# Transposing the probabilities ahead of the next unit's scores in a two-layer diffusion trunk

## The reference

```python
s_win = where(valid, einsum('bnqkgd,bnskd->bnkgqs', qb, kb) * scale, -inf)
s_ctx = einsum('bnqkgd,bckd->bnkgqc', qb, kc) * scale
p = softmax(concatenate([s_sink, s_ctx, s_win], axis=-1), axis=-1)
o = einsum('bnkgqc,bckd->bnqkgd', p_ctx, vc) + einsum('bnkgqs,bnskd->bnqkgd', p_win, vb)
```

## Time and profile before

| | |
|---|---|
| median of 3 runs | 1605.48 us (1605.39 to 1608.4) |
| the profiled execution | 1605.48 us, its span 1603.8 us |
| TensorE busy with matmuls | 1527.6 us, 95% of the span |
| TensorE busy with weight loads | 967.7 us, 60% |
| VectorE | 679.4 us, 42% |
| ScalarE | 314.5 us, 20% |
| GpSimd | 38.5 us, 2% |
| DMA | mean 230 GB/s |

### The profile page before, as it was taken

The page is one execution under the profiler, slowest core; times in us unless marked ns, Lnnn a source line. Parts: engine busy times, 40 slices in busy tenths (PEclk is TensorE's granted clock), DMA queues, the critical chain, the costliest instruction groups (busy, mean ns, idle before and its releaser), DMA issues. The chain is left out here.

```text
span 1603.8 us, 23021 instructions
## 1 busy us (share of the span) xinstructions
PE 1527.6 (95%) x9610; PEld 967.7 (60%) x9610; DVE 679.4 (42%) x1400; ACT 314.5 (20%) x721; POOL 38.5 (2%) x49
## 2 busy tenths in 40 slices
PE   5999989999999999989999999999999999899995
PEld 2764644754445446875556556776678888655553
DVE  1396776556655433451222126345533312611112
ACT  2121144321121100110111013234322111100011
POOL 0000000000000000000000020000000000000000
PEclk7999999999999999999999999999999999999998
DMA  9575411524525349379999986332115368899996
GB/s 367 186 242 180 140 43 53 133 69 142 185 92 180 138 172 355 139 278 402 411 396 395 401 344 226 114 99 67 40 43 168 127 254 314 312 426 429 420 410 289
DMA packets 127816, 368.08 MB, mean 230 GB/s; under 512 B 14237, under 2 KB 91319, under 8 KB 106972
## 3 DMA queue, kind: packets, MB, share of 16 engines
q1 hardware_dynamic: 118588, 344.86, 57.0%
q10 hardware_dynamic: 5392, 10.99, 2.3%
q0 software_dynamic: 3728, 10.71, 1.8%
HBM read 355.89 MB, written 12.98 MB: 230 GB/s over the span
## 5 line engine op out<-in xcount | busy, mean ns | idle before, releaser
L1304 PE MATMUL ps<-hT,ring 128*128 128x512 f32 (+1 forms) x768 | 258.5, 486 | 1.4 <-ACT arena L1774 1.4
L1177 PE MATMUL ps<-hT,ring 128*128 128x512 f32 (+1 forms) x544 | 207.7, 535 | 0.0
L1304 PEld LDWEIGHTS ps<-hT,ring 128*128 128x128 f32 x768 | 144.1, 190 | 98.1 <-issue 88.7
L1180 PE MATMUL ps<-ring,hT 128*128 128x256 f32 (+1 forms) x832 | 173.5, 365 | 6.5 <-DVE arena L2083 5.0
L1180 PEld LDWEIGHTS ps<-ring,hT 128*128 128x128 f32 x832 | 146.9, 190 | 30.6 <-issue 13.5
L1177 PEld LDWEIGHTS ps<-hT,ring 128*128 128x128 f32 x544 | 101.4, 191 | 87.1 <-issue 82.0
L1321 PE MATMUL ps<-arena,ring 128*128 128x512 f32 (+1 forms) x384 | 132.7, 486 | 0.0
L1467 PE MATMUL ps<-ring,arena 128*32 128x128 f32 (+2 forms) x1216 | 107.5, 343 | 2.8 <-DMA ring<-in_w_exp_gate 2.3
L1321 PEld LDWEIGHTS ps<-arena,ring 128*128 128x128 f32 x384 | 72.3, 190 | 47.8 <-issue 43.1
L1467 PE MATMUL ps<-arena 128*32 128x128 f32 (+1 forms) x1264 | 91.7, 328 | 1.9 <-DMA arena<-in_w_exp_up 1.2
L1467 PEld LDWEIGHTS ps<-ring,arena 128*32 128x32 f32 (+2 forms) x1216 | 66.5, 128 | 41.8 <-issue 24.8
(11 more groups left out here) (288 smaller groups left out, 1593.6 us busy)
## 6 DMA issues: line engine op xcount, KB each, us to landing
ring<-in_w_in SPq DMA_DIRECT2D x54, 1024.0 KB, 6.2
ring<-in_w_ada SPq DMA_DIRECT2D x48, 1024.0 KB, 5.1
arena<-in_w_exp_down SPq DMA_DIRECT2D x18, 2048.0 KB, 19.0
arena<-in_w_exp_up SPq DMA_DIRECT2D x15, 2048.0 KB, 17.2
ring<-in_w_exp_down SPq DMA_DIRECT2D x14, 2048.0 KB, 16.9
ring<-in_w_exp_gate SPq DMA_DIRECT2D x12, 2048.0 KB, 18.0
ring<-in_w_exp_up SPq DMA_DIRECT2D x12, 2048.0 KB, 17.0
hT<-in_w_exp_gate SPq DMA_DIRECT2D x10, 2048.0 KB, 18.3
```

The costliest lines, as they stand in the source:

```text
L1177: last = pe.matmul(ps[:, bank, 0:tok.stop - tok.start], w[:, k, at:at + width], hT[:, k, tok], start=(k == 0), stop=(k == KD - 1))
L1180: last = pe.matmul(ps[:, bank, 0:width], hT[:, k, P * tok:P * (tok + 1)], w[:, k, at:at + width], start=(k == 0), stop=(k == KD - 1))
L1304: last = pe.matmul(ps[:, 0, lo:TOK], kview(n)[:, k, P * (m % 2):P * (m % 2 + 1)], hT[:, k, lo:TOK], start=(k == 0), stop=(k == KD - 1))
```

## The change

In TensorE's `unit(n)` the transposes of unit n-1 now stand ahead of the scores of unit n. In VectorE's `unit(n)` the copy of those transposes (`keep_turned`) now stands ahead of the maxima. Nothing else is changed: no wait, no buffer, no plan. ScalarE's, GpSimd's and SyncE's programs are the same instruction for instruction.

```diff
@@ TensorE, unit(n)
                     if 2 <= n:
                         outputs(n - 2)
+                    if 1 <= n <= n_units[l]:
+                        turn(n - 1)
                     if n < n_units[l]:
                         scores(n)
-                    if 1 <= n <= n_units[l]:
-                        turn(n - 1)
@@ VectorE, unit(n)
                     if 2 <= n:
                         keep_output(n - 2)
+                    if 1 <= n <= n_units[l]:
+                        keep_turned(n - 1)
                     if n < n_units[l]:
                         maxima(n)
-                    if 1 <= n <= n_units[l]:
-                        keep_turned(n - 1)
```

## The result

The changed kernel is slower: 1620.05 us median of five runs (1618.65 to 1625.72), against 1608.4 of the kernel before on the same chips (1605.39 to 1610.51). The ratio is 1.0082, with a 95% interval of 1.0067 to 1.0096, some 13 us. The forecast was 1611.6 us in a range of 1606.5 to 1615.5. The sign was right. The size was less than half of what came, and the time lies outside the range.

What follows compares the result with a forecast made beforehand. The prediction took TensorE, busy 1527.6 of 1603.8 us, as the bound. Waits for the divide 4.95, bank copies 0.4 and 0.8 made 6.15 us on 1605.48: 1611.6 us, range 1606.5 to 1615.5.

Steps and rivals of the forecast that it cites:

- What bounds the kernel, and where the change acts: TensorE, busy 1527.6 of 1603.8 us, sets the end; the change acts in layer 0's `b` units, where transposes wait 5.4 us.
- Term s: Scores that filled TensorE's wait for the divide now follow it: 0.7 us with 256 keys, 1.1 with 512.
- term d: VectorE's copy ahead of the maxima makes the divide later: 0.35 us per unit with 256 keys, 0.6 with 512, adding up.
- The forecast's eight waits: Layer 0 transposes waiting for the divide at b0, b2, b3, b5, b6, b7, b9, b10, making TensorE 4.95 us later.
- Where the divide is long done, the two just change places and cost nothing.: In units whose transposes don't wait for the divide, swapping them with the scores costs TensorE nothing.
- the zero for the `a` units: TensorE has no wait in layer 0's `a` units and the copy's delay is hidden, so the change costs zero there.
- The forecast's own sign for layer 1: If layer 1 adds more than 1.5 us, its slack was smaller than the forecast took it for.
- The bank copies: TensorE waits longer for VectorE's copy L2083 because the maxima come later: 0.4 us at b13, 0.8 in layer 1.
- I keep one fall, as today.: TensorE's clock falls to half once, at b3, as before; a fall more or less at b7 is 1.5 us of range.
- One swap only: Rival, chance 0.17: VectorE's copy stays hidden, lateness doesn't add up, only b7's 1.1 us remains after b0; 1606.6 us.
- Faster: Rival, chance 0.04: VectorE's copy fits its idle time before the maxima, waits for L2083 go, -4.1 us; 1601.4 us.
- Lateness feeds itself: Rival, chance 0.15: second clock fall at b7, longer one at b3, bank copies in every late unit; 1614 to 1617 us.

Runs made afterwards that it cites:

- The kernel with the slack units alone: Changed order on both engines only in layer 0's `a` units and all layer 1 units, against the kernel before: ratio 1.0019, 3.1 us slower.

## Why the prediction was wrong

**What bounds the kernel, and where the change acts.** Right. TensorE's lateness in the mixers went to the end whole; the experts between neither absorbed nor added more than 1 us in the two profiles.

**Term s behind a wait, and term d.** Right in place and nearly in size. The forecast's eight waits came, the other eight units had none, and TensorE's idle time in the stretch grew by 4.5 us, where the waits were to bring 4.95 and 0.4. For d the mechanism is only half right. The forecast took it from the copy's new place ahead of the maxima. With the copy left in its old place the waits were 10.4 instead of 10.9 us: what the forecast had as a tie, ScalarE's copies waiting for TensorE's late projection, then makes the divide late by nearly as much. That the sum of d came out is therefore in part luck. At b0 the forecast had overlooked a wait of the scores for the exponentials (1.3 us) ahead of the one for the divide. In the changed kernel both are one wait of 2.38 us, which left the end of it where it was computed but made a single long idle stretch.

**"Where the divide is long done, the two just change places and cost nothing."** This step failed, and with it the zero for the `a` units. Each swap of a `b` unit costs 0.19 us, where weight loads are exposed, whether anything waits or not. The kernel with the slack units alone shows it: 1.8 us in layer 1's `b` stretch, of which 0.4 are the waits for L2083 that were forecast, and 0.6 and 0.45 in the `a` stretches. (The forecast's own sign for layer 1, more than 1.5 us there, came true, with 2.25; it read it as less slack, but it was the borders.) What it is that costs in the `a` units is not shown: there the scores ahead of the outputs cost 0.66 and 0.28 as well. In all some 5.5 us that had no term; with them the sum would have been 11.65 us and the forecast 1617.1, above its range. The rows were in sight: the forecast weighed pulling ahead of weight loads only across a wait, and not at the borders where it goes on in every unit, under the transposes at 304.76. The Trainium skill's page "TensorE: Matmul & The Clock Gate", section "Step-by-step: what each phase is for", says that a load can run ahead if its row group doesn't conflict or if it goes to the background buffer. Here full-height loads do run ahead under full-height matmuls (304.76, ahead of the matmul at 304.87). Next to products of 64 rows they did not (314.05 and 315.11).

**The bank copies.** 0.2 to 0.3 us at b13 and 0.4 in layer 1, against 0.4 and 0.8 forecast: right in kind, a little too large.

**"I keep one fall, as today."** Mis-sized, and the bound too narrow. The profile of the changed kernel has three falls in the stretch and loses 3.4 us more by them than before. But another profile of the same stretch has two, and the old order's stretch also fell to 0.97 in one of four profiles and ranged over 3 us. The forecast should have treated the clock as something that varies between executions, not as a row of the one profile.

**The rivals.** "One swap only" fell: the lateness did add up, and it did so even where VectorE's copy stayed put. "Faster" fell: the maxima start at 315.23, right behind the scores' end (315.19), and the scores themselves come 1.0 us later in the unit, so the copy's place brought nothing. "Lateness feeds itself" named the clock, but its other source, bank copies in every late unit, did not come. It is the nearest in size for partly the wrong reason.

## What to carry to other kernels

When work is swapped on TensorE, price the borders: look at whether the next weight load starts under the matmul before it, and keep full-height work between partial-height products and the stream that follows. The step that waits belongs behind work that doesn't, and here moving it by one matmul in the other direction gained 3 us, part of it through the clock, while two or three matmuls in every unit gained nothing or lost; the copies behind it have to move in their engine's queue as well. Compare stretches cut at the same instructions at equal granted clock before a difference is put down to the change.

## What the runs showed of the hardware

A weight load next to a product of 64 rows was exposed: the border of transposes to scores took 0.2 us from matmul to matmul where transposes follow each other in 0.11, and the projection's first product behind the scores took 0.1 us longer than behind transposes. In otherwise identical `b` stretches the granted clock was 0.99 in three profiles and 0.97 in one, for 3.0 us of difference. Where the wait of b3 was filled with throw-away transposes the clock stayed whole (1.00 over 228 to 238 us), but in the same profile it fell behind b0's waits, where another execution had kept it, and behind waits of 1.44 and 0.51 us at b5: the stretch as a whole was granted 0.98.
